# The seam between the MLP's up and down phases: loads, places and residual in another order

## The reference

```
xn2 = rmsnorm(x, norm_mlp)                                  # (1088, 1024)
x   = x + square(relu(xn2 @ w_up)) @ w_down                 # w_up (1024, 4096), w_down (4096, 1024)
y   = rmsnorm(x, norm_final)
```

## Time and profile before

| | |
|---|---|
| median of three runs | 1690.45 us (1689.87 to 1691.78) |
| profiled execution | 1691.79 us |
| its span | 1690.0 us |
| TensorE (PE) busy | 1625.9 us, 96% |
| VectorE (DVE) busy | 1067.4 us, 63% |
| ScalarE (ACT) busy | 600.7 us, 36% |
| GpSimd (POOL) busy | 541.9 us, 32% |
| mean granted TensorE clock | 0.987 |
| up phase's last product starts | 1293.21 us |
| down phase's first product starts | 1297.43 us |

### The profile page before, as it was taken

One profiled execution on the slowest core, in us unless ns is written; L12 is line 12 of the kernel. 1 busy time (PEld: TensorE's weight loads), 2 busy tenths in 40 slices (PEclk: granted clock), 3 DMA queues, 4 the chain that ended last, 5 costly groups with the idle time before them and its releaser, 6 DMA issues.

```text
span 1690.0 us, 23816 instructions
## 1 busy us (share of the span) xinstructions
PE 1625.9 (96%) x9377; PEld 1408.4 (83%) x9377; DVE 1067.4 (63%) x1618; ACT 600.7 (36%) x1274; POOL 541.9 (32%) x409
## 2 busy tenths in 40 slices
PE   9999999999999999999998799999998899999996
PEld 8998998999998899889887588888886677777774
DVE  5413323442155345663637988888886688888888
ACT  6423333332245333552305422222222444444422
POOL 3002001100002100210003555566661466666664
PEclk9999999999999999999999899999999899999998
DMA  6115354453312123112423143333336444444312
GB/s 216 52 35 131 61 71 92 67 71 42 56 27 50 42 51 70 26 26 46 148 50 125 56 150 137 137 137 134 124 130 253 166 130 135 137 137 138 123 40 106
DMA packets 158345, 165.93 MB, mean 98 GB/s; under 512 B 83722, under 2 KB 129810, under 8 KB 156186
## 3 DMA queue, kind: packets, MB, share of 16 engines
q1 hardware_dynamic: 158232, 164.41, 34.9%
HBM read 121.46 MB, written 44.63 MB: 98 GB/s over the span
## 4 chain that ended last, share of the span: by engine, by line
PE 71%; DVE 9%; issue 3%; POOL 3%; DMA 2%; ACT 2%; SPq 1%; DVEq 0%; POOLq 0%; ACTq 0%
PE bank L1123 28%; PE bank L1532 18%; PE bank L1571 7%; PE bank L1475 5%; PE bank L1068 2%; DVE a_lo_S L2709 2%; PE bank L1497 2%; DVE t_f L2733 2%; PE bank L1309 2%; POOL e L3108 2%; PE bank L1279 1%; DMA raw<-in_w_in 1%; DVE acc L2760 1%; POOL w_lo L3121 1%; DMA a_f_S<-hid_dram 1%
## 5 line engine op out<-in xcount | busy, mean ns | idle before, releaser
L1123 PE MATMUL bank<-xT_hi,w_hi 128*128 128x384 f32 (+1 forms) x1008 | 194.2, 334 | 0.7 <-ACT w_hi L1650 0.7
L1123 PE MATMUL bank<-xT_hi,w_lo 128*128 128x384 f32 (+1 forms) x1008 | 186.2, 326 | 0.0
L1123 PE MATMUL bank<-xT_lo,w_hi 128*128 128x384 f32 (+1 forms) x1008 | 186.1, 326 | 0.0
L1123 PEld LDWEIGHTS bank<-xT_hi,w_hi 128*128 128x128 f32 x1008 | 166.5, 188 | 5.2 <-issue 3.9
L2202 DVE TENSOR_TENSOR w_lo<-raw,w_hi 128x1024 fp32r<-128x1024 f32 (+1 forms) x54 | 70.4, 1304 | 157.2 <-ACT w_hi L1650 157.0
L1123 PEld LDWEIGHTS bank<-xT_lo,w_hi 128*128 128x128 f32 x1008 | 168.7, 188 | 0.0
L1123 PEld LDWEIGHTS bank<-xT_hi,w_lo 128*128 128x128 f32 x1008 | 168.7, 188 | 0.0
L3041 POOL TENSOR_SCALAR_AFFINE_SELECT pT<-pT 128x512 f32<-128x512 f32 x32 | 22.4, 700 | 308.4 <-ACT pT L1845 308.4
L1532 PE MATMUL bank<-xT_hi,w_hi 128*128 128x512 f32 x256 | 101.7, 397 | 4.1 <-issue 4.1
L1532 PE MATMUL bank<-xT_lo,w_hi 128*128 128x512 f32 x256 | 101.4, 396 | 0.0
L1729 ACT ACTIVATE sig<-bank 128x384 f32<-128x384 f32 (+1 forms) x72 | 34.0, 473 | 172.8 <-PE bank L1123 172.7
(11 more groups left out here) (369 smaller groups left out, 3930.7 us busy)
## 6 DMA issues: line engine op xcount, KB each, us to landing
hid_dram<-hst SPq DMA_DIRECT2D x15, 1792.0 KB, 5.7
raw<-in_w_in SPq DMA_DIRECT2D x64, 256.0 KB, 4.6
raw<-in_w_up SPq DMA_DIRECT2D x16, 1024.0 KB, 5.3
a_f_S<-hid_dram SPq DMA_DIRECT2D x29, 512.0 KB, 3.7
a_f_A<-hid_dram SPq DMA_DIRECT2D x24, 512.0 KB, 3.8
raw<-in_w_in SPq DMA_DIRECT2D x9, 1024.0 KB, 5.8
raw<-in_w_down SPq DMA_DIRECT2D x8, 1024.0 KB, 5.2
b_f<-in_w_down SPq DMA_DIRECT2D x8, 1024.0 KB, 7.7
```

Of the source, the lines that this page charges most:

```text
L1123: last = nc.tensor.matmul(out, lhsT, rhs, start=(step == 0), stop=(step == 3 * KT - 1))
```

## The change

- The loads of B1 and B2 for block 0 move ahead of the store of group 14. B1 waits for the last group's weight sums and rests (`u_sum`, `u_bl`), B2 for its T rests (`u_tl`), and the store stands behind both.
- The slots are laid out anew: S4, S1, A11 in `sx_hi`; S3, A22, A12 in `sx_lo`; `b1_first` in S3's upper half. A11 and A12 now lie in the place of form S4, which P3 reads: their loads wait for P3, not for P6.
- SyncE's order behind them: S4 behind P6; `acc1` and `acc8` behind P5; S1, A22, `acc2` and S3 behind P7; the last store; S2.
- `acc2` has a semaphore of its own, `x2_back_b`. DVE and POOL wait for `acc1` and `acc8` only (`x2_back`, 32) ahead of block 0, and POOL waits for `acc2` ahead of its subtraction in it.
- DVE: in the last group U2 is joined ahead of the `b1_first` rest; the sampled rest goes ahead of T1's sum; S1's rest goes ahead of P3's adds (before: behind A22's rest). ACT rounds S1 ahead of A22. The lists of orders follow.

The computation stays the same.

```diff
 def rounded_forms():
-    out = [(x, 0) for x in ("B1", "B2", "A11", "A12", "smp", "S4", "T1", "T2", "T4", "T3", "A22", "S1")]
+    out = [(x, 0) for x in ("B1", "B2", "A11", "A12", "smp", "S4", "T1", "T2", "T4", "T3", "S1", "A22")]
...
 def dve_forms():
-    out = [(x, 0) for x in ("B11", "A11", "A12", "+T1", "+T2", "+T4", "B21", "smp")]
+    out = [(x, 0) for x in ("B11", "A11", "A12", "smp", "+T1", "+T2", "+T4", "B21")]
...
-        out += [("T3", b), ("A22", b)] + ([("S1", 0)] if first else []) + ([("S2", 0)] if first else []) + [("S3", b)]
+        out += [("T3", b)] + ([("S1", 0)] if first else []) + [("A22", b)] + ([("S2", 0)] if first else []) + [("S3", b)]
...
-            for name in ("A11", "S4", "S1", "A12", "A22"):
+            for name in ("S4", "S1", "A11"):
                 a_slot(name)
             with ExitStack() as s2:
                 a2 = scope_alloc(s2)
                 a2("under_b1_first", [P, 2, HT])
                 b1_first = a2("b1_first", [P, 2, HT], F32R)
-            a_slot("S3")
+            for name in ("S3", "A22", "A12"):
+                a_slot(name)
...
             for g in range(1, NG):
                 if g + 1 < NG:
                     up_dma(g + 1)
+                else:
+                    sp.wait_ge(u_sum, 4 * NG)
+                    sp.wait_ge(u_bl, 2 * NG)
+                    load_b(0, 0)
+                    sp.wait_ge(u_tl, 2 * NG)
+                    load_b(0, 1)
                 store_hidden(g - 1)
-            sp.wait_ge(u_sum, 4 * NG)
-            sp.wait_ge(u_bl, 2 * NG)
-            load_b(0, 0)
-            sp.wait_ge(u_tl, 2 * NG)
-            load_b(0, 1)
             sp.wait_ge(hid_out[0], 16)
             sp.wait_ge(hid_out[1], 16)
             sp.wait_ge(x2_out, 16 * NT)
-            sp.wait_ge(u_mm, up_made(LAST, "P6"))
+            sp.wait_ge(u_mm, up_made(LAST, "P3"))
             load_a(0, "A11")
             load_a(0, "A12")
+            sp.wait_ge(u_mm, up_made(LAST, "P6"))
+            load_a(0, "S4")
             sp.wait_ge(u_mm, up_made(LAST, "P5"))
             sp.dma_start(acc1[:, :, :], x2_dram[0:HB].rearrange("i p c -> p i c")).then_inc(x2_back, 16)
-            sp.dma_start(acc2[:, :, :], x2_dram[HB:2 * HB].rearrange("i p c -> p i c")).then_inc(x2_back, 16)
             sp.dma_start(acc8[0:NS, :], x2_dram[NT - 1, 0:NS, :]).then_inc(x2_back, 16)
+            sp.wait_ge(u_mm, up_made(LAST, "P7"))
             load_a(0, "S1")
+            load_a(0, "A22")
+            sp.dma_start(acc2[:, :, :], x2_dram[HB:2 * HB].rearrange("i p c -> p i c")).then_inc(x2_back_b, 16)
             load_a(0, "S3")
-            sp.wait_ge(u_mm, up_made(LAST, "P7"))
-            load_a(0, "S4")
-            load_a(0, "A22")
             store_hidden(LAST)
...
+            round_a(0, "S1")
             round_a(0, "A22")
-            round_a(0, "S1")
...
-                else:
+                join(g, "U2")
+                if g + 1 == NG:
                     dve.wait_ge(d_rnd, ROUNDED["B1", 0])
                     nc.vector.tensor_tensor(b1_first[:, :, :], dn_raw("B11"), dn_w("B11", False).bitcast(F32),
                                             ALU.subtract).then_inc(d_dve, 1)
-                join(g, "U2")
...
+            rest_smp(0)
             sum_t(0, "T1")
             sum_t(0, "T2")
             sum_t(0, "T4")
             rest_b(0, "B21")
-            rest_smp(0)
-            dve.wait_ge(x2_back, 48)
+            dve.wait_ge(x2_back, 32)
...
+                if b == 0:
+                    rest_a(0, "S1")
                 add_stage(b, "P3")
                 rest_a(b, "A22")
-                if b == 0:
-                    rest_a(0, "S1")
...
                 else:
-                    pool.wait_ge(x2_back, 48)
+                    pool.wait_ge(x2_back, 32)
...
                 if b == 0:
+                    pool.wait_ge(x2_back_b, 16)
                     v = acc2[:, :, 0:HD2]
```

More of the change, by code:

```diff
@@ L589, in layer_kernel @@
         x2_back = sem("x2_back")
+        x2_back_b = sem("x2_back_b")
         sx_4 = sem("sx_4")
```

## The result

| | before | changed |
|---|---|---|
| median | 1690.45 us (4 runs, 1689.87 to 1691.78) | 1678.15 us (4 runs, 1677.65 to 1681.22) |
| ratio, 95% interval | 1 | 0.993 (0.9917 to 0.9942) |
| profiled execution, span | 1691.79, 1690.0 us | 1677.65, 1675.9 us |
| mean granted TensorE clock | 0.987 | 0.989 |

A forecast was written before the change was run, and what follows sets the result against it. TensorE, busy 1625.9 of 1690.0 us, was the bound, leaving 15.8 us of seam waits and its clock to win. P6 12.1 us sooner takes 1691.79 to 1679.7 us; the median, 1.34 lower, is 1678.4 us, range 1672 to 1684.

The forecast's parts named there:

- Loads and DVE's chain: Start of the seam: B1, B2 landed by 1272 and 1282, A11 costs 0.4 us, T1's sum at 1297.6 for 1303.16.
- P2: TensorE ahead of P2 in block 0: a 2.7 us wait for B21 replaces the earlier 3.2 us wait.
- P3 and the turns with POOL: Ahead of P3, DVE and POOL alternate whole operations, costing 5.5 us; P3 starts at 1315.8 for 1320.11.
- P3's clock: TensorE in P3, behind 6.4 us of idling: a slow start charged at 2.9 us.
- S1 and P5: S1's rest, ahead of P3's adds, done at 1323.7; P5 starts at 1326.1 without waiting, its 2.9 us slow start gone.
- The residual: Residual loads behind S4: S4 lands near 1292, is rounded by 1295.3, and ACT's 14.73 us wait is gone.
- The sum: Start of P6: 1331.7 for 1343.57, 11.9 us sooner, 12.1 with S2's half chance; the end moves by the same.
- rival 1: Ahead of P3, DVE and POOL meet only once, over B12; P3 starts at 1312.5, 1673 to 1675 us; chance 0.17.

The follow-up runs named there:

- e6: Changed kernel with the A11 and A12 loads waiting for P6 again and the sampled rest behind B21's again; 1679.89 us, ratio 0.9932.
- e1: Changed kernel plus one wait: in block 0 POOL starts its B12 rest only when DVE has made the S4 rest; 1673.12 us, ratio 0.9892.
- e10: The changed kernel itself run once more, unaltered; 1678.72 us, ratio 0.9929.
- e7: Changed kernel with S1's rest behind P3's adds and A22's rest again, ACT rounding A22 ahead of S1; 1684.73 us, ratio 0.9955.
- e4: Changed kernel with acc1, acc2, acc8 loaded ahead of S4, S1, A22, S3, and DVE and POOL waiting for all three; 1678.06 us, ratio 0.9929.
- e8: Kernel before the change with only the B1 and B2 loads moved ahead of the store of group 14; 1689.01 us, ratio 0.9983.
- e5: Changed kernel with the B1 and B2 loads behind the store of group 14 again; 1684.82 us, ratio 0.9961.
- e3: Changed kernel with block 0 in order of due time and POOL's block 1 A11 rest held until S2 is made; 1676.71 us, ratio 0.9915.

## Why the prediction was right, point by point

**Loads and DVE's chain.** T1's sum was forecast 4.4 us behind the last up product (1297.6 less 1293.21) and came at 4.36; before it was at 10.0. A11 cost nothing, 0.4 was charged. Its landing:

```profile
hid_dram<-hst SPq DMA_DIRECT2D x1, 1792.0 KB, 7.0
...
a_f_A<-hid_dram SPq DMA_DIRECT2D x1, 512.0 KB, 6.8
```

The store issued at 1278.47 landed at 1285.5, A11 at 1286.8, 1.3 behind it: the order of the queue held. That it matters for A11 and A12 to wait for P3 and not for P6, which the prediction took for granted, is not borne out: e6.

**P2.** Forecast was a wait of 2.7 us; it was 2.3. What I left out is that the clock falls behind it: P2 with its sampled products ran 8.1 us from 1300.80 to 1308.9 instead of 6.5. It cost nothing, because P3 waited for DVE anyway: the wait ahead of P3 was 4.2 for a forecast of 6.4, and its end 0.5 us sooner than forecast. A term was left out here, and it was luck that the next wait covered it.

**P3 and the turns with POOL.** Forecast 22.6 us behind the last up product, measured 22.1; without the turns the sum would have been 16.7, and e1, which takes POOL out of DVE's way, has P3 at 16.7. This step decided the forecast, and e1 shows it. The prediction had four of POOL's operations ahead of S4's rest, B12 and three adds, and so has the trace. What the Trainium skill calls an exclusive lock (SBUF — State Buffer, SBUF: two separate sides) is what the rows of this case look like, the 0.42 us rest that took 4.86 beside POOL's subtraction above all. The rows show the turns; what makes them they do not show.

**P3's clock.** 2.9 us charged, 2.7 measured (8.33 us for 24 products), 1.6 in e10. What decides between the two was not tried.

**S1 and P5.** S1's rest was forecast at 1323.7, 30.5 us behind the up phase, and came at 29.8. That P5 would not wait was right, within the 0.4 us of e10. The prediction gave this move no price of its own; e7 shows that it carries about as much as the early down loads.

**The residual.** That ACT's 14.73 us would be gone is true and was worth nothing by itself: e4. The wait was the longest of ACT's in the seam, but in e4, where 10 us of it are back, what it holds up misses POOL's operations instead of meeting them.

**The sum.** P6 was forecast 38.5 us behind the last up product (1331.7 less 1293.21) and came at 37.9; behind P6 the time is the same within 0.5 us, as forecast. That the total agrees to 0.2 us is partly luck: the first point above alone scatters over 3.5 us from profile to profile.

**The parts together.** Alone, the down loads gave 3.1 us at P6 (e8); undone from the whole they cost 4.8 (e5), S1's order 6.2 (e7), the residual's order nothing in the times (e4, whose profile has P6 4.6 us sooner), the two small moves 0.2 (e6). Such numbers need not add up to the 12.4 us of the whole: the down loads give less alone than they cost when undone, because in e8 the next wait, for the residual and S4, stands behind them. Of the rivals none came true. In e4 ACT's late copies miss S4's rest, as rival 1 had it, but B12 misses it too: that is no meeting at all, with DVE waiting for ACT, and P3 comes at 19.6 where e1 has 16.7.

**Open.** Why the rate falls ahead of `acc8`'s landing was not tried. It is a load into 64 of the 128 partitions, where those around it fill all; the changed kernel (250 and 240 GB/s from 1294 to 1296, `acc8` landing at 1296.5) and e4 (303 and 205 from 1300 to 1302, landing at 1302.6) show the dip too, but no run here has the load in another shape. How e4's profile can be 4.6 us better in the seam than the changed kernel's while the medians agree is left open too; its runs scatter over 6.4 us.

## What to carry to other kernels

A stall that is shortened lets the work behind it move up, and two engines that had been apart can meet: before counting a stall as won, lay the timelines of DVE and POOL over each other at their new times and let them take turns, a whole operation each. When they meet on the critical chain, a wait that holds the less urgent engine back can be worth more than another early load (5 us here for one line; the early down loads gave 3 alone). A wait of TensorE behind which the clock falls can cost almost the same again, 2.8 us on top of 3.2 in e7.

## What the hardware did that I had not expected

- A 2.3 us wait ahead of P2 was followed by a stretch at 1.2 GHz (0.75 mean from 1300 to 1304, 0.50 from 1302 to 1304), while before the change 3.2 us ahead of the sampled products was not (1.00 from 1308 to 1312); e1 has the same 2.3 us wait, and a clock of 1.00 in the 4 us behind it, and in e6 and e8 the same 3.2 us are followed by 0.50. Length of a wait alone does not say whether the clock falls.
- The smallest operation can pay as much as a large one: 128x256 elements on DVE, 0.42 us alone, took 4.86 us beside a 5.62 us operation of POOL's (e3), 4.4 more than alone; the 128x1024 rest of S1 paid 3.8 beside the subtraction in the changed kernel.
- The point at which the seam begins scattered over 3.5 us between profiles, though up to there TensorE runs the same products and none of the edits moves a wait of its. Of a change of 12 us, that is over a quarter, if it isn't taken out.
